# Reordering the independent products around a long convolution: where weight splits and four modulation blocks stand

## The reference

```python
h = rmsnorm(x, g_norm1) * (1.0 + sc1) + sh1            # sh1, sc1, gt1, sh2, sc2, gt2 = modulation(c)
k, v, a, u, q, r, hy, gate = split_cols(h @ w_in)
...
z = x1 * long_conv_bidir(v, h[:, 0], h[:, 1], bias[0])     # Hyena: two long convolutions by FFT, one after the other
y_hy = x2 * long_conv_bidir(z, h[:, 2], h[:, 3], bias[1])
...
m = sigmoid(g_hy) * (y_hy @ w_hy) + sigmoid(g_gla) * (y_gla @ w_gla) + sigmoid(g_s5) * (y_s5 @ w_s5)
x = x + gt1 * (m @ w_out)
h2 = rmsnorm(x, g_norm2) * (1.0 + sc2) + sh2
x = x + gt2 * swiglu(h2, w_ffn_in, w_ffn_out)
return rmsnorm(x, g_final)
```

## Time and profile before

| what | value |
|---|---|
| median of three runs | 1220.31 us (1219.78 to 1221.37) |
| the profiled execution | 1222.88 us, its span 1221.1 us |
| TensorE matmul busy | 1112.5 us, 91% of the span |
| VectorE busy | 589.4 us, 48% |
| ScalarE busy | 401.3 us, 33% |
| GpSimd busy | 335.2 us, 27% |
| mean granted TensorE clock | 0.946 of full speed |

### The profile page before, as it was taken

One profiled execution on the slowest core, in us unless ns is written; L12 is line 12 of the kernel. 1 busy time (PEld: TensorE's weight loads), 2 busy tenths in 40 slices (PEclk: granted clock), 3 DMA queues, 4 the chain that ended last, 5 costly groups with the idle time before them and its releaser, 6 DMA issues.

```text
span 1221.1 us, 15749 instructions
## 1 busy us (share of the span) xinstructions
PE 1112.5 (91%) x6109; PEld 847.9 (69%) x6109; DVE 589.4 (48%) x1135; ACT 401.3 (33%) x763; POOL 335.2 (27%) x288
## 2 busy tenths in 40 slices
PE   4799989978989999998997979798999999999995
PEld 1368948866667676777473654697888888888884
DVE  3775156576598888883196966445000012000013
ACT  2762323443344544432411100234323212232221
POOL 2032212501300000000131210352655545665540
PEclk9899989988989998998998989898999999999998
DMA  9820223765222223313323237561333233333211
GB/s 316 270 103 27 70 69 130 130 150 174 69 61 87 88 70 71 86 58 101 144 86 120 69 109 260 178 183 48 104 104 92 73 94 104 104 104 104 78 44 70
DMA packets 139367, 134.32 MB, mean 110 GB/s; under 512 B 12937, under 2 KB 125865, under 8 KB 138268
## 3 DMA queue, kind: packets, MB, share of 16 engines
q1 hardware_dynamic: 126448, 105.52, 29.5%
q0 software_dynamic: 3744, 16.15, 3.6%
q10 hardware_dynamic: 9100, 11.64, 3.2%
HBM read 120.18 MB, written 11.01 MB: 107 GB/s over the span
## 4 chain that ended last, share of the span: by engine, by line
PE 56%; DVE 13%; issue 3%; ACT 2%; DMA 1%; ACTq 1%; POOL 0%; DVEq 0%; POOLq 0%
PE psum L746 49%; PE psum L1006 1%; PE psum L1109 1%; PE psum L986 1%; DMA buf<-in_w_out 1%; PE psum L779 1%; DVE ring_lo L2056 1%; PE psum L999 1%; DVE buf L2132 1%; ACTq L1582 1%; DVE hT_lo L2395 1%; PE psum L974 1%; DVE buf L2102 1%; DVE buf L2309 1%; DVE buf L2105 1%
## 5 line engine op out<-in xcount | busy, mean ns | idle before, releaser
L1298 POOL TENSOR_TENSOR ring_lo<-buf,ring_hi 128x512 fp32r<-128x512 f32 (+2 forms) x220 | 282.1, 1314 | 504.9 <-ACT ring_hi L1453 504.9
L746 PE MATMUL psum<-hT_hi,ring_hi 128*128 128x512 f32 x712 | 286.8, 403 | 8.7 <-DVE hT_lo L2395 4.0
L746 PE MATMUL psum<-hT_lo,ring_hi 128*128 128x512 f32 x712 | 280.2, 394 | 0.0
L746 PE MATMUL psum<-hT_hi,ring_lo 128*128 128x512 f32 x712 | 279.9, 393 | 0.0
L1453 ACT ACTIVATE ring_hi<-buf 128x512 fp32r<-128x512 f32 (+1 forms) x260 | 139.6, 610 | 227.7 <-PE psum L746 161.6
L746 PE MATMUL psum<-buf,buf 128*128 128x512 f32 (+1 forms) x368 | 152.2, 570 | 21.9 <-issue 15.4
L746 PEld LDWEIGHTS psum<-hT_hi,ring_hi 128*128 128x128 f32 x712 | 135.7, 191 | 42.6 <-issue 5.4
L746 PEld LDWEIGHTS psum<-hT_lo,ring_hi 128*128 128x128 f32 x712 | 135.9, 191 | 28.7 <-issue 1.7
L746 PEld LDWEIGHTS psum<-hT_hi,ring_lo 128*128 128x128 f32 x712 | 135.4, 190 | 29.1
L746 PEld LDWEIGHTS psum<-buf,buf 128*128 128x128 f32 x368 | 68.9, 207 | 94.3 <-issue 85.4
L2404 DVE TENSOR_TENSOR buf<-psum,buf 128x512 f32<-128x512 f32 x22 | 15.2, 692 | 221.5 <-PE psum L746 221.5
(11 more groups left out here) (333 smaller groups left out, 1694.0 us busy)
## 6 DMA issues: line engine op xcount, KB each, us to landing
buf<-in_w_in SPq DMA_DIRECT2D x26, 1024.0 KB, 5.1
buf<-in_w_mod SPq DMA_DIRECT2D x24, 1024.0 KB, 8.2
buf<-in_w_ffn_in SPq DMA_DIRECT2D x44, 512.0 KB, 5.1
buf<-in_w_ffn_out SPq DMA_DIRECT2D x8, 1024.0 KB, 5.0
scr_k<-buf POOLq DMA_DIRECT2D x4, 1024.0 KB, 5.5
buf<-scr_k POOLq DMA_DIRECT2D x4, 1024.0 KB, 7.9
buf<-in_w_out SPq DMA_DIRECT2D x4, 1024.0 KB, 6.6
buf<-in_w_ffn_out SPq DMA_DIRECT2D x4, 768.0 KB, 4.6
```

The source lines that it names most:

```text
L746: ins = nc.tensor.matmul(o, a, b, start=start and n == 0, stop=stop and n == len(pairs) - 1)
L1298: nc.gpsimd.tensor_tensor(ring_lo[:, a:a + n], ring[:, a:a + n], ring_hi[:, h + i * n:h + i * n + n].bitcast(fp32), SUB)\
```

## The change

The independent products stand in another order, and the modulation blocks of gt1 and gt2 are taken apart from their `gt` steps. Blocks 8 and 9 now stand between the first convolution and the second forward transform, where gate product (0, 3, 0) stood. Blocks 10 and 11 stand ahead of the second inverse transform. The gate products of branch 0 with block `gate03` move behind those of `gate22`. One gate product and one branch product of block 3 of branch 2 move behind the second inverse. Rows 10 and 11 get buffers of their own in `restart`, a table that the earlier scans used. The bias loads are issued ahead of the load of x and have their own semaphore.

```diff
@@ -291,6 +291,8 @@
+        gate_row = {i: mrow[i % 2] for i in (8, 9, 20, 21, 22, 23)}
+        gate_row[10], gate_row[11] = restart[:, 0:256], restart[:, 256:512]
@@ -563,13 +565,22 @@
         evs = [ms[0](), ms[2]()]
-        beside = [ms[1], ms[3]] + kept[4:6] + ms[4:8] + kept[6:8] + ms[8:]
+        beside = [ms[1], ms[3]] + kept[4:6] + ms[4:12] + kept[6:8] + ms[12:]
...
+        gates = [8, 9, 10, 11, 20, 21, 22, 23]
+        made = []
+
+        def mod_row():
+            i = gates.pop(0)
+            want(f"mod{i}", block(w_mod, 256 * i), split=False)
+            step("mod", i)
+            made.append(i)
@@ -585,39 +596,38 @@
             step("uunfold", cv)
+            if cv == 0:
+                one_beside()
+                step("yinv", cv)
+                one_beside(False)
+                mod_row()
+                mod_row()
+            else:
+                one_beside(False)
+                mod_row()
+                mod_row()
+                step("yinv", cv)
+                one_beside()
+        while beside:
             one_beside()
-            step("yinv", cv)
-            one_beside()
-        while late or beside:
-            one_beside()
-            one_beside()
...
         beside = ms0
         for n in range(8):
             one_beside()
             if n > 2:
-                mod_gate()
+                step("gt", made.pop(0))
+            if n > 5:
+                mod_row()
...
             step("wo", i)
-            mod_gate()
+            if gates:
+                mod_row()
+            if made:
+                step("gt", made.pop(0))
...
+                    pool.dma_start(bgt[0], I["b_mod"][0][2 * D:3 * D].partition_broadcast(P)).then_inc(S("gate_bias"), 16)
+                    pool.dma_start(bgt[1], I["b_mod"][0][5 * D:6 * D].partition_broadcast(P)).then_inc(S("gate_bias"), 16)
                     pool.dma_start(xr, I["x"][0].rearrange("(t p) d -> p t d", p=P)).then_inc(ld, 16)
```

More of the change, by code:

```diff
@@ L615, in hybrid_block @@
             step("wo", i)
-            mod_gate()
+            if gates:
+                mod_row()
+            if made:
+                step("gt", made.pop(0))
             if i == 0:
                 step("A2")
-        while made:
-            mod_gate()
         step("h2T")
@@ L800, in gt_rows @@
                 o = open_job(name)
-                close(nc.tensor.matmul(o[:, 0:256], pick[:, 0:1].to_broadcast([P, P]), mrow[i % 2],
+                close(nc.tensor.matmul(o[:, 0:256], pick[:, 0:1].to_broadcast([P, P]), gate_row[i],
                                        start=True, stop=True), name)
@@ L1361, in yinv @@
                     ld = S("p4_load")
+                    pool.dma_start(bgt[0], I["b_mod"][0][2 * D:3 * D].partition_broadcast(P)).then_inc(S("gate_bias"), 16)
+                    pool.dma_start(bgt[1], I["b_mod"][0][5 * D:6 * D].partition_broadcast(P)).then_inc(S("gate_bias"), 16)
                     pool.dma_start(xr, I["x"][0].rearrange("(t p) d -> p t d", p=P)).then_inc(ld, 16)
-                    pool.dma_start(bgt[0], I["b_mod"][0][2 * D:3 * D].partition_broadcast(P)).then_inc(ld, 16)
-                    pool.dma_start(bgt[1], I["b_mod"][0][5 * D:6 * D].partition_broadcast(P)).then_inc(ld, 16)
                     pool.dma_start(gfin, I["g_final"].partition_broadcast(P)).then_inc(ld, 16)
@@ L1798, in mod @@
                 o = full(dve, f"mr{i}")
-                V.tensor_copy(mrow8[i] if i < 8 else mrow[i % 2], o[:, 0:256]).then_inc(freed(f"mr{i}"), 1)
-                if i >= 8:
+                row = mrow8[i] if i < 8 else gate_row[i] if i in gate_row else mrow[i % 2]
+                V.tensor_copy(row, o[:, 0:256]).then_inc(freed(f"mr{i}"), 1)
+                if i >= 8 and i not in (8, 9, 10, 11):
                     last_T[i % 2] = f"mod{i}" if 12 <= i < 20 else f"gt{i}"
@@ L2356, in gt_rows @@
                 if i == 8:
-                    dve.wait_ge(S("p4_load"), 64)
+                    dve.wait_ge(S("gate_bias"), 32)
                 name = f"gt{i}"
@@ L2373, in wo @@
                     o = full(dve, name)
+                    if i + t == 0:
+                        dve.wait_ge(S("p4_load"), 32)
                     c = slice(256 * i, 256 * i + 256)
```

## The result

The changed kernel takes **1207.84 us** in the median of four runs (1203.47 to 1210.28), against 1220.05 (1218.12 to 1221.37, four runs) of the kernel before on the same chip: a ratio of 0.9909, 95% interval 0.9889 to 0.9928. The ratio is estimated from all runs and is not the quotient of the two medians, which is 0.9900. The kernel is faster: by 12.2 us by the medians and by 11.1 us (8.8 to 13.5) by the ratio, where 7.2 were forecast. The profiled execution of the changed kernel took 1203.47 us, its span 1201.7. It was the fastest of its runs, and that of before (1222.88) was slower than its median; so I compare stretches inside the traces, and not the two spans.

What follows compares the result with a forecast made beforehand. TensorE, busy 91% of the span, was taken as the bound, waiting on VectorE's chain, which GpSimd's splits slow. Gains of 10.8 and 1.0 us against losses elsewhere summed to -7.2, so 1220.3 becomes 1213.1 us; range 1205.0 to 1217.7.

Steps and rivals of the forecast that it cites:

- F: Stretch from the first forward transform to the second: 63.0 us before, forecast 52.2.
- G: Stretch from the second forward transform to the second inverse: 47.5 us before, forecast 48.2.
- H: Stretch from the second inverse to the output projection: 61.3 us before, forecast 65.2.
- A: Main case, as summed: gate03's collision gone, the other two stay; 1213.1 us, within 1210.5 to 1215.5; chance 0.52.
- rival B: Splits meet no SBUF-only work, or VectorE holds the ports: gate22 2.8 us better, gate23 4.4, both 1205.9; chance 0.24.
- The collisions: GpSimd splits beside VectorE's SBUF-only uunfold operations: gate22's in the first, gate23's in the second, +4.4 us each.
- The second convolution: Second forward transform to its inverse: old collision -4.2, gate23's +4.4, gate03's spill-over +0.5, so 47.5 becomes 48.2 us.
- From the second inverse to the projection: 61.3 us plus 8.9 for two products, -3.0 for three mod, +0.5 for a gt, -2.5 of wait: 65.2.
- Behind the projection: Between the four blocks of the projection one mod less, -1.0 us; nothing of the feed-forward part moves.
- C: Gate22's split holds one first-uunfold operation for 5.6 us and the clock falls: 4.6 us worse, 1217.7; chance 0.12.
- D: Ends where it began: C, and the projection's wait stays 6.6 us: 1220.2; chance 0.07.
- E: Slower: gate22 comes too late for its use behind the second forward transform, costing the 7.2 us gain and more; chance 0.05.

Runs made afterwards that it cites:

- before again: The kernel before, with no edit, run and profiled a second time: 1218.48 us, ratio 1.0008 to the kernel before.
- after again: The changed kernel, with no edit, run and profiled a second time: 1209.28 us, ratio 0.9922 to the kernel before.
- the waits: Changed kernel with GpSimd's split of gate22 or gate23 held until that convolution's uunfold is done: 0.9903 and 0.9878 alone, 0.9872 both, against the kernel before.
- the kernel before with waits: The kernel before, nothing moved, with GpSimd's splits of gate03 and gate22 held until the first uunfold is done: 1209.25 us, ratio 0.9916.
- the kernel with the modulation blocks back: The changed kernel with modulation blocks 8 to 11 back beside branch 0's products: 1217.76 us, ratio 1.0002 to the kernel before.

## Why the prediction was right, and where its sizes were off

The stretch got 10.7 us shorter where 6.2 were forecast. The 4.5 us between them are 1.2 in F, 0.3 in G and 2.9 in H. The median of 1207.84 lies below A's own 1210.5 to 1215.5 and among the times of rival B, yet the traces show A's collisions: A was right in its mechanism and too cautious in its sizes.

**The collisions.** Right in kind and place. For `gate22` the prediction had the load's issue 35.7 us after the first forward transform and GpSimd 41.6 after it; measured were 632.94 (35.7) and 639.00 (41.8). It said that the *last four* operations collide, +4.4. By its own numbers the fifth operation begins at 646.3, ahead of GpSimd's 646.6, and could have been left out. Three did collide: the fifth had begun at 638.63, 0.37 us ahead of GpSimd, and kept its 0.68. The chain to `yinv`'s reads took 5.0 us from 639.24, where three normal steps take 1.8, so 3.2 us were lost instead of 4.4. That is the 1.2 us by which F fell further (12.0 us instead of 10.8). What taking the collision away gives back is 1.7 us, not 3.2: with normal steps TensorE's own 7.1 us of inverse set the pace. For `gate23` the prediction had the split 37.5 us into the second convolution and +4.4; it came at 37.7 and cost 4.1.

**The second convolution**: 47.5 - 4.2 + 4.4 + 0.5 = 48.2 forecast, 47.87 measured. The spill-over of `gate03`'s split was one operation of 1.16 us at 658.12, 0.5. The step that I did not see is the order's own cost, masked in the sum: before there are also two pairs of evacuations in this chain (692.10 and 706.31), and the order could have taken one out.

**From the second inverse to the projection** the sum gave 65.2 and the trace 62.25, the largest miss. The inverse itself began at half clock (granted 0.50 from 696 to 698) and took 8.78 us in this execution, 10.23 before; in the other programs it took 8.73 to 10.19, so these 1.5 us are scatter. Without the inverse's own time H is 51.06 before and 53.47 after, 2.4 more where the terms of the prediction make 3.9. The missing 1.5 are in small terms. The wait for a modulation load (0.32) is gone. The projection waits 3.84 and not 4.1. And a branch product with its `gt` takes 3.87 us now (740.07 to 743.94), where with a `mod` beside it I had 3.53 + 0.53; three such pairs stand there, 0.6 together. Another 0.3 I did not trace. VectorE's last product ends the wait, as said.

**Behind the projection** I had -1.0. From the projection to the span's end it is 443.4 us against 444.3, but from 441.7 to 444.3 over all kernels. The four with the list of before have 443.4 to 444.3, the seven with the moved blocks 441.7 to 443.8, which fits the sign; the size is not shown.

**What the rows could not give** is the time of everything ahead of the stretch. The medians differ by more than the stretches in one session (12.2 us) and by less in the other (8.1). By the ratios it is 11.1 and 9.5 us, and both intervals (8.8 to 13.5, 6.8 to 12.2) hold the stretch's 10.7, so the excess in the first session may be luck. The part up to the first forward transform takes 597.2 to 605.0 us in the profiled executions of all kernels shown here, whose programs are alike there, and kernels in the old arrangement (599.9 to 605.0) don't stand apart from the others (597.2 to 604.5). Within it TensorE's waits for modulation loads (9.3 us before, 8.9 before again, 7.0 after, 9.7 after again) and the granted clock from 250 to 300 us (0.83, 0.83, 0.90, 0.83) differ; what decides them I didn't find.

**Rivals.** *B*, by a split without an SBUF-only partner, did not happen, and its price was right for `gate23`: its 4.4 is 4.1 on the chip. For `gate22` it had 2.8, and it is 1.7. Its other half, that VectorE wins a collision and loses nothing, did not happen either: the two collisions that were left cost 1.7 and 4.1 us, as the waits show. The traces do show who goes first. Operations in flight when a split began kept their 0.68 us (638.63 and 685.57 here, 682.22 in the kernel before), and each one behind them waited its turn, at steps of 1.67 to 1.69 us (639.24 to 644.27). This nearly agrees with what the Trainium skill states ("SBUF — State Buffer", "Who interferes with whom": who issues first takes the shared pair for the whole instruction and the other blocks), if it is taken one instruction at a time: a VectorE step of 0.60 and a GpSimd piece of 1.24 (4.96 by 4) would then take 1.84 together. Read so, the rule makes no collision of several operations free for VectorE, though the prediction priced it that way; and two of the three collisions before (628.28 and 682.38) fit it. What the rule does not give are the three held operations of the last section, which had begun first and still waited. *C* and *D* needed one operation held for 5.6 us in the first `uunfold`; none was. *E* needed a wait on `gate22`; there was none.

**Where F's 12.0 us came from**, one step after the other (in another order the shares may differ): taking the gate product out of the place behind the first inverse gives 7.4 (63.0 to 55.6, which removes the whole-hold of 5.59 us too), keeping the split out of the middle of the convolution 7.1 (to 48.5), two modulation blocks cost 0.8 (to 49.3) and the collision in `uunfold` 1.7 (to 51.0).

## What to carry to other kernels

Read a list order as a list of load issues as well: the modulation blocks earned part of their gain by taking ring places, which delayed a split out of a bad overlap. Where a helper engine's work has slack, a wait on the critical engine's counter holds it out of the overlap at little cost (1.53 us of waiting for a low part in the kernel before, none in the changed kernel). Two lines of it gave as much here as the reordering, and 5.8 us of the stretch more on top of it. And price a collision by what it sets off: 4.1 us of waiting brought 3.0 of half clock with it, while a collision near TensorE's own pace cost half of its length.

## What the runs showed of the hardware

**Two ways to collide.** In most overlaps VectorE and GpSimd take turns: VectorE's SBUF-only operations take 1.5 to 1.8 us instead of 0.68 and GpSimd's four pieces 6.4 to 6.8 instead of 4.9 to 5.0. In three executions one VectorE operation was held until all four pieces were done, and these kept their pace. The kernel before, again, VectorE and GpSimd:

```profile
644.26 5.58 DVE L2309 TENSOR_TENSOR buf<-buf 128x512 f32<-128x512 f32 x1
649.77 0.68 DVE L2310 TENSOR_TENSOR buf<-buf 128x512 f32<-128x512 f32 x1
```

```profile
643.26 1.09 POOL L1337 DMA_DIRECT2D buf<-scr_k  x2 [13.67 <-DVEq L1771]
644.37 4.92 POOL L1298 TENSOR_TENSOR ring_lo<-buf,ring_hi 128x512 fp32r<-128x512 f32 x4
```

The held operation began 0.11 us ahead of GpSimd's first piece here and in the earlier trace rows, and 0.26 ahead in the kernel before with waits (651.09, held 5.85). How far ahead it began does not decide this. In the kernel with the modulation blocks back an operation began 0.09 us ahead and kept its 0.68, and turns followed; so it was with 0.16 and 0.17 us in the kernel before, its second profile and the kernel before with waits (682.22 against 682.38 in the first), and with 0.30 to 0.49 elsewhere. VectorE and GpSimd with the modulation blocks back:

```profile
681.57 0.68 DVE L2341 TENSOR_TENSOR buf<-buf 128x512 f32<-128x512 f32 x1
682.18 1.76 DVE L2342 TENSOR_TENSOR buf<-buf 128x512 f32<-128x512 f32 x1
```

```profile
681.66 6.82 POOL L1306 TENSOR_TENSOR ring_lo<-buf,ring_hi 128x512 fp32r<-128x512 f32 x4 [12.78 <-ACT ring_hi L1461]
```

What sets the three held cases apart in these traces is that GpSimd came straight from a DMA issue, without waiting for ScalarE. Whether that is the cause was not tried.

**The SBUF-only steps of an evacuation feel it too.** In the kernel after, `wo0`'s split of 6.04 us at 749.98 stretches a cast of one SBUF operand from 0.43 to 1.38 us; VectorE's timeline:

```profile
746.48 0.43 DVE L2201 CAST mT_hi<-buf 128x512 fp32r<-128x512 f32 x1
...
751.83 1.38 DVE L2201 CAST mT_hi<-buf 128x512 fp32r<-128x512 f32 x1
```
